# Scores of two prompt chunks from one stationary key tile per level, with the second chunk's keys and values in turned order

## What is computed

```python
def step(S, inp):
    qc, kc, vc, gc = inp
    b = jnp.cumsum(gc, axis=2)
    diff = b[:, :, :, None, :] - b[:, :, None, :, :]
    decay = jnp.exp(jnp.where(causal, diff, -jnp.inf))
    scores = jnp.einsum('bhtk,bhsk,bhtsk->bhts', qc, kc, decay)
    o = (jnp.einsum('bhts,bhsv->bhtv', scores, vc)
         + jnp.einsum('bhtk,bhkv->bhtv', qc * jnp.exp(b), S))
    b_last = b[:, :, -1:, :]
    S = (jnp.exp(b_last[:, :, 0, :])[..., None] * S
         + jnp.einsum('bhsk,bhsv->bhkv', kc * jnp.exp(b_last - b), vc))
    return S, o
```

## Time and profile before

| | us |
|---|---|
| median of 3 runs | 1489.78 (1488.51 to 1493.13) |
| the profiled execution, its own time | 1493.66 |
| span of that execution | 1491.4 |
| TensorE busy | 1460.7 |
| VectorE busy | 804.9 |
| ScalarE busy | 550.8 |
| GpSimd busy | 188.2 |

### The profile page before, as it was taken

How to read it: one execution, slowest core, us unless ns; L and a number is a source line. 1 busy time by engine, 2 the same in 40 slices (tenths; PEclk the granted TensorE clock), 3 DMA queues, 4 the chain that set the end, 5 groups by cost and what they waited for, 6 DMA issues and landing times.

```text
span 1491.4 us, 27027 instructions
## 1 busy us (share of the span) xinstructions
PE 1460.7 (98%) x9928; PEld 1440.6 (97%) x9928; DVE 804.9 (54%) x1200; ACT 550.8 (37%) x823; POOL 188.2 (13%) x202
## 2 busy tenths in 40 slices
PE   7999999999999999999999999999999999999996
PEld 5999999999999999999999999999999999999996
DVE  4657788787665554444444444444444444444443
ACT  6443433344443343333333333333333333333443
POOL 0244434333112210000000000000000000000131
PEclk9999999999999999999999999999999999999998
DMA  8445444434455555554565555565554556555453
GB/s 222 136 127 143 128 127 131 114 114 138 114 162 143 153 144 153 141 160 125 146 187 142 141 142 141 144 164 153 157 141 134 151 146 164 154 151 141 119 148 114
DMA packets 409519, 214.52 MB, mean 144 GB/s; under 512 B 4093, under 2 KB 407757, under 8 KB 409420
## 3 DMA queue, kind: packets, MB, share of 16 engines
q1 hardware_dynamic: 391207, 203.52, 49.8%
q10 hardware_dynamic: 18277, 10.52, 2.5%
HBM read 206.14 MB, written 7.89 MB: 144 GB/s over the span
## 4 chain that ended last, share of the span: by engine, by line
PE 85%; DVE 9%; issue 3%; ACT 2%; DMA 1%; DVEq 0%; ACTq 0%; SPq 0%
PE bank L366 27%; PE bank L367 27%; PE bank L368 27%; DVE qr L1190 2%; DVE w_lo L1013 2%; DVE t L1177 1%; ACT w_hi L682 1%; DVE sc L1205 1%; PE bank L507 1%; DMA xt<-in_x_sample 1%; DVE sn L1249 0%; PE bank L462 0%; PE bank L410 0%; PE bank L538 0%; PE bank L412 0%
## 5 line engine op out<-in xcount | busy, mean ns | idle before, releaser
L366 PE MATMUL bank<-a_hi,w_hi 128*128 128x320 f32 x2048 | 642.4, 314 | 0.0
L367 PE MATMUL bank<-a_lo,w_hi 128*128 128x320 f32 x2048 | 636.1, 311 | 0.0
L368 PE MATMUL bank<-a_hi,w_lo 128*128 128x320 f32 x2048 | 635.9, 311 | 0.0
L1013 DVE TENSOR_TENSOR w_lo<-w_raw,w_hi 128x1024 fp32r<-128x1024 f32 (+1 forms) x416 | 467.3, 1164 | 150.3 <-ACT w_hi L682 149.5
L682 ACT ACTIVATE w_hi<-w_raw 128x1024 fp32r<-128x1024 f32 (+1 forms) x416 | 387.3, 967 | 158.6 <-PE bank L368 148.5
L366 PEld LDWEIGHTS bank<-a_hi,w_hi 128*128 128x128 f32 x2048 | 387.6, 189 | 2.4
L367 PEld LDWEIGHTS bank<-a_lo,w_hi 128*128 128x128 f32 x2048 | 387.7, 189 | 0.8
L368 PEld LDWEIGHTS bank<-a_hi,w_lo 128*128 128x128 f32 x2048 | 387.3, 189 | 0.0
L366 PE MATMUL bank<-h_hi,w_hi 128*128 128x320 f32 x704 | 217.7, 309 | 0.0
L367 PE MATMUL bank<-h_lo,w_hi 128*128 128x320 f32 x704 | 216.6, 308 | 0.0
L368 PE MATMUL bank<-h_hi,w_lo 128*128 128x320 f32 x704 | 216.5, 308 | 0.0
(11 more groups left out here) (218 smaller groups left out, 1186.5 us busy)
## 6 DMA issues: line engine op xcount, KB each, us to landing
w_raw<-in_w_gate SPq DMA_DIRECT2D x44, 1024.0 KB, 5.6
w_raw<-in_w_up SPq DMA_DIRECT2D x44, 1024.0 KB, 5.6
w_raw<-in_w_down SPq DMA_DIRECT2D x64, 704.0 KB, 4.8
w_raw<-in_w_in SPq DMA_DIRECT2D x39, 1024.0 KB, 5.8
w_raw<-in_w_o SPq DMA_DIRECT2D x16, 1024.0 KB, 6.1
s<-in_state_hgrn ACTq DMA_DIRECT2D x8, 512.0 KB, 4.3
out<-sn ACTq DMA_DIRECT2D x8, 512.0 KB, 7.2
xt<-in_x_prompt SPq DMA_DIRECT2D x3, 512.0 KB, 9.4
```

The costliest lines, as they stand in the source:

```text
L366: pe.matmul(out, whi[:, par_, cols], r_hi, start=(k == 0), stop=False)
L367: pe.matmul(out, whi[:, par_, cols], r_lo, start=False, stop=False)
L368: last = pe.matmul(out, wlo[:, par_, cols], r_hi, start=False, stop=(k == last_k))
L1013: dve.tensor_tensor(wlo[:, par_, cols], raw[:, par_, cols], whi[:, par_, cols].bitcast(F32), SUB)\
```

## The change

The second chunk's keys and values are kept in turned (reversed) order, by GpSimd (`second_turned` in `keys`) and VectorE (`turned`, in place of one `scaled` into `vv`). In the turned chunk the first block of each pair comes second, so the 64 valid key columns of chunk 0 and the 64 of chunk 1 fill one tile of 128 columns without overlap. A new tile `km[l]` holds them. TensorE makes one product per level, `km[l]` stationary and 128 query columns moving, in place of two with 64. The mask table holds turned rows for chunk 1, and the put on the diagonal takes a turned identity from `cst`. GpSimd now keeps prompt keys in one tile `kp` that is multiplied in place, in the first blocks only (the second blocks' factor was 1), and the sample tokens' keys in `ks[l]`.

```diff
@@ rec_scores on TensorE
                 def level(bk, at, l):
-                    for c in range(NC):
-                        last = pe.matmul(bk[:, at + c * 64:at + c * 64 + 64].rearrange("p (m j) -> p m j", j=2 ** l),
-                                         kx[l][:, c * CH:(c + 1) * CH], right_half(qr[l][:, c * CH:(c + 1) * CH], l),
-                                         start=True, stop=True)
-                    return last
+                    return pe.matmul(bk[:, at:at + P].rearrange("p (m j) -> p m j", j=2 ** l),
+                                     km[l][:, :], right_half(qr[l][:, 0:TP], l), start=True, stop=True)
@@ the value projection on VectorE
+            def turned(n, par_):
+
+                done(n)
+                z = zb[par_]
+                dve.tensor_tensor(vv[:, 0:CH], z[:, 0:CH], rbc[:, 0:CH], MUL)
+                dve.tensor_tensor(second_turned(vv), z[:, CH:TP], rbc[:, CH:TP], MUL)
+                return dve.tensor_tensor(vv[:, TP:N], z[:, TP:N], rbc[:, TP:N], MUL)
...
-                    scaled(n + 2, par_, vv[:, :]).then_inc(unit_read, 1)
+                    turned(n + 2, par_).then_inc(unit_read, 1)
@@ keys on GpSimd
-                pool.tensor_tensor(kx[0][:, :].rearrange("p (m a) -> p m a", a=2),
-                                   ones[:, 0:1].unsqueeze(2).to_broadcast([P, N // 2, 2]), tl[0][:, :, 1:3], SUB)\
-                    .then_inc(kx_ready, 1)
+                spans = [(lambda ap: ap[:, 0:CH], 0, CH, 0), (second_turned, CH, CH, 1)]
+                for part, t0, n in [s[:3] for s in spans] + [(lambda ap: ap[:, TP:N], TP, NS)]:
+                    last = pool.tensor_tensor(part(kx0).rearrange("p (m a) -> p m a", a=2),
+                                              ones[:, 0:1].unsqueeze(2).to_broadcast([P, n // 2, 2]),
+                                              tl[0][:, t0 // 2:(t0 + n) // 2, 1:3], SUB)
+                last.then_inc(kx_ready, 1)
                 for l in range(LP):
-                    n = N if l < LS else TP
+                    src, m = (kp if l else kx0), CH // 2 ** (l + 1)
+                    one = ones[:, 0:1].unsqueeze(2).to_broadcast([P, m, 2 ** l])
                     pool.wait_ge(kx_ready, (LP + 1) * h + l + 1)
+                    for c in range(NC):
+                        last = pool.tensor_tensor(half_of(km[l][:, :], l, c), half_of(src[:, c * CH:(c + 1) * CH], l, c),
+                                                  one, MUL)
+                    last.then_inc(km_ready, 1)
                     if l:
                         pool.wait_ge(prod_ready, LP * h + l)
-                    pool.tensor_tensor(blocks_of(kx[l + 1], l, n), blocks_of(kx[l], l, n), times(l, n, 2), MUL)\
-                        .then_inc(kx_ready, 1)
+                        pool.wait_ge(km_ready, LP * h + l + 1)
+                    for part, t0, n, c in spans:
+                        if l:
+                            firsts = half_of(part(kp), l, 0)
+                            last = pool.tensor_tensor(firsts, firsts,
+                                                      tl[l][:, c * m:(c + 1) * m, 2:3].to_broadcast([P, m, 2 ** l]), MUL)
+                        else:
+                            last = pool.tensor_tensor(blocks_of(part(kp), 0, CH), blocks_of(part(kx0), 0, CH),
+                                                      times(0, CH, 2, t0), MUL)
+                    if l < LS:
+                        last = pool.tensor_tensor(blocks_of(ks[l + 1], l, NS), blocks_of(ks[l], l, NS),
+                                                  times(l, NS, 2, TP), MUL)
+                    last.then_inc(kx_ready, 1)
```

More of the change, by code:

```diff
@@ L54 @@
 C_ID = 0
-C_MP = C_ID + P
+C_AI = C_ID + P
+C_MP = C_AI + P
 C_MS = C_MP + LP * P
@@ L81, in constant_table @@
         for ch in range(NC):
-            c[:, C_MP + level * P + ch * 64:C_MP + level * P + ch * 64 + 64] = m
+            c[:, C_MP + level * P + ch * 64:C_MP + level * P + ch * 64 + 64] = m[::-1] if ch else m
         if level < LS:
@@ L162, in hybrid_kernel @@
         qr = region(early, [(f"qr{l}", [P, N if l <= LS else TP], F32) for l in range(LP + 1)])
-        kx = region(early, [(f"kx{l}", [P, N if l <= LS else TP], F32) for l in range(LP + 1)])
+        kx0, kp = region(early, [("kx0", [P, N], F32), ("kp", [P, TP], F32)])
+        km = region(early, [(f"km{l}", [P, CH], F32) for l in range(LP)])
+        ks = [kx0[:, TP:N]] + [t[:, :] for t in region(early, [(f"ks{l}", [P, NS], F32) for l in range(1, LS + 1)])]
         junk, = passing([("junk", [P, 1024], BF16)])
@@ L214, in hybrid_kernel @@
             sem(n) for n in ("pool_mm", "mp_hi_s", "mp_lo_s", "st_tr", "st_copied", "out_done"))
-        zf_sig, f_ready, prod_ready, zq_sig, q_ready, qr_ready, kx_ready = (
+        zf_sig, f_ready, prod_ready, zq_sig, q_ready, qr_ready, kx_ready, km_ready = (
             sem(n) for n in ("zf_sig", "f_ready", "prod_ready", "zq_sig", "q_ready",
-                             "qr_ready", "kx_ready"))
+                             "qr_ready", "kx_ready", "km_ready"))
         v_tr, k_tr, vt_ready, kt_ready, vm_ready, sc_mm, sc_put, put_go = (
@@ L259, in blocks_of, with times @@
             return ap[:, 0:n].rearrange("p (m a j) -> p m a j", a=2, j=2 ** level)
-        def times(level, n, lo):
-            m = n // 2 ** (level + 1)
-            return tl[level][:, 0:m, lo:lo + 2].unsqueeze(3).to_broadcast([P, m, 2, 2 ** level])
+        def times(level, n, lo, t0=0):
+            m, m0 = n // 2 ** (level + 1), t0 // 2 ** (level + 1)
+            return tl[level][:, m0:m0 + m, lo:lo + 2].unsqueeze(3).to_broadcast([P, m, 2, 2 ** level])
         def prod_in(level, which):
@@ L269, in prod_in, with second_turned, half_of @@
             return tl[level][:, 0:m, which:which + 1].rearrange("p (m a) q -> p m (a q)", a=2)
+        def second_turned(ap):
+            return ap[:, CH:TP][:, ::-1]
+        def half_of(ap, level, a):
+            return ap.rearrange("p (m a j) -> p m a j", a=2, j=2 ** level)[:, :, a, :]
         def right_half(ap, level):
@@ L513, in rec_scores @@
                 last.then_inc(sc_mm, 1)
[L514 to L517, removed]
+                for c, own in enumerate((kx0[:, 0:CH], kx0[:, CH:TP])):
+                    pe.matmul(SA[:, c * CH:(c + 1) * CH], own, qq[:, c * CH:(c + 1) * CH], start=True, stop=True)
+                last = pe.matmul(SA[0:NS, TP:N], ks[0], qq[:, TP:N], start=True, stop=True)
                 for l in range(LS):
                     last = pe.matmul(SA[0:NS, N + 32 * l:N + 32 * l + 32].rearrange("p (m j) -> p m j", j=2 ** l),
-                                     kx[l][:, TP:N], right_half(qr[l][:, TP:N], l), start=True, stop=True)
+                                     ks[l], right_half(qr[l][:, TP:N], l), start=True, stop=True)
                 last.then_inc(sc_mm, 1)
@@ L1320, in window @@
                     done(n + 2)
-                    out, src = thrice(v_rep, zb[par_])
-                    dve.tensor_tensor(out, src, thrice(v_rep, rbc)[1], MUL).then_inc(v_thrice, 1)
-                    scaled(n + 2, par_, vv[:, :]).then_inc(unit_read, 1)
+                    out, src = thrice(v_rep, zb[par_][:, TP:N])
+                    dve.tensor_tensor(out, src, thrice(v_rep, rbc[:, TP:N])[1], MUL).then_inc(v_thrice, 1)
+                    turned(n + 2, par_).then_inc(unit_read, 1)
                 else:
@@ L1508, in key_copies @@
                 after(pool, obc_mm, h)
-                out, src = thrice(k_rep, kx[LS])
+                out, src = thrice(k_rep, ks[LS])
                 one = ones[:, 0:2].unsqueeze(2).unsqueeze(3).to_broadcast([P, 2, 3, HS])
```

11 lines of the change are left out of this document (6 added, 5 removed).

## The result

The changed kernel takes 1505.05 us (median of 4 runs, 1503.06 to 1506.13) against 1491.45 (4 runs, 1488.51 to 1493.17): 1.0092 of the time before, with an interval of 1.0069 to 1.0114. It is slower by 0.9%, some 13.6 us, where 3.9% and 59 us were forecast (1549, with a range of 1508 to 1577). The measured time lies 3 us under the lower end of that range. The profiled execution of after has a span of 1502.1 us, 10.7 more than that of before.

What follows compares the result with a forecast made beforehand. VectorE and ScalarE in turns were taken to set the steady heads' period. Seven periods at 7.7 us gave 54, plus 6.7 for the first head, minus 1.3 on TensorE: +59 us on 1489.8, so 1549, range 1508 to 1577.

Steps and rivals of the forecast that it cites:

- The saving of 1.3 us a head on TensorE: TensorE's level products: 1.1 to 1.6 us saved a head, hidden in holes except in the last head, -1.3 us.
- the 0.15 us for `vv`: VectorE: one `vv` of 320 columns becomes three; two more instructions cost 0.15 us a head, on the path.
- the one from `kx0` to `q_ready` at 262.9: GpSimd's chain from keys to query tile: `q_ready` at 262.9, so VectorE starts `queries` 6.7 us later than at 256.18.
- The price of a short step: GpSimd's multiplies: 0.36 us on 64 columns, 0.16 us per own wait; levels 1 to 6 and `qq` 12.2 us.
- What stands in the way: VectorE's `t`, `w_lo` and norm steps hold up GpSimd from level 1 to `qq`, about 4 us.
- The start of level 1: GpSimd's `kx0` and level 0 fill 241.32 to 246.7; level 1 begins at 246.7, when `products` has its first result.
- relief for VectorE: VectorE's steps beside GpSimd's shorter ones: no gain was counted.
- sn in the queries: GpSimd's `k_rep` and `sn` both fall into VectorE's `queries`, 0.8 us a head more.
- the slow stretch: TensorE's lower clock behind its longer waits: 0 to 1 us a head, taken as 0, with 8 us kept for range.
- TensorE's waits: TensorE's holes grow to some 5 us ahead of the diagonal (L397) and 5 ahead of the level products.
- The milder rival: GpSimd's short steps cost 0.15 to 0.2 us, `q_ready` at 258 to 259, 1508 to 1520; chance 0.18.
- the hidden rival's condition: GpSimd's 26 added steps and 7 waits must cost under 2.5 us together; then 1479, chance 0.04.

Runs made afterwards that it cites:

- run 3: Changed kernel with GpSimd's query (`qq`) issued ahead of level 4 of keys, not behind level 6: 1467.02 us, ratio 0.9828.
- run 4: Changed kernel with copies into `km` on level 0 alone, TensorE using `km[0]` on every level (scores not the reference's): 1479.25 us, ratio 0.9913.
- run 5: Kernel before with GpSimd's eight key steps cut into 36 of 64 columns, nothing left out: 1515.03 us, ratio 1.0168.
- run 8: Changed kernel with query ahead of level 4 and each level's product cut back into two of 64 columns: 1484.2 us, ratio 0.9947.
- run 6: Kernel before with one added wait, so GpSimd's `sn` starts after VectorE's first put of that head: 1480.89 us, ratio 0.9925.
- run 7: Changed kernel with an added wait so `sn` starts after VectorE's first put, query left in place: 1491.1 us, ratio 0.999.
- run 1: Kernel before with one 128-column product per level, chunk 0's keys serving both chunks (scores not the reference's): 1486.93 us, ratio 0.9967.
- run 2: Changed kernel with each level's product cut back into two of 64 query columns on the same `km` tile: 1520.55 us, ratio 1.0194.
- run 10: Changed kernel with query ahead of level 4 and `sn` behind VectorE's first put: 1466.75 us, ratio 0.9825.

## Why the prediction was wrong, and where it was right

**Right: the direction and the mechanism.** `qq` became late, VectorE waited for it in every head, 2.6 us in the steady ones and 6.0 in the first, and short steps on GpSimd are the cause (runs 3, 4, 5). The saving of 1.3 us a head on TensorE was sized rightly (run 8), and so were the 0.15 us for `vv`.

**Wrong: the size.** The step that failed is the one from `kx0` to `q_ready` at 262.9. A head was to cost 7.7 us: 6.7 for `q_ready`, 0.8 for `sn` and `k_rep` in `queries`, 0.15 for `vv`. A steady head cost 1.4, and the mean of the seven was 1.1. Laid on the forecast's clock, `q_ready` came at 257.3 (16.0 us behind the start of `keys`, not 21.6). These 5.6 us are made up of three parts:
- *The price of a short step, 3.2 us.* 0.36 us for 64 columns was taken from a line through 192 and 320 columns. Measured: 0.28. The wait between own steps was taken at 0.16; it was 0.08 here. A level of four steps took 1.28 us and not 1.76. From level 1 to `qq` this is 9.0 us of work, and not 12.2.
- *What stands in the way, 1.7 us.* 4 us were forecast behind level 1 for VectorE's steps; it was 2.3 (2.7 in the head shown first). The two pieces of `w_lo` cost 1.8 to 1.9, near the forecast's 2.0, but the short norm steps next to nothing (0.16 us at 225.04, in the midst of GpSimd's steps) and `products` some tenths.
- *The start of level 1, 0.7 us.* Its first key step began 4.7 us behind the start of `keys` and not 5.4.

**A term at nothing: relief for VectorE.** Shorter instructions on one engine shorten the other's waits, since each waits for a whole instruction of the other. It was 1.1 to 1.3 us a head in `products` and 1.3 in the weight rests (mean 1276 ns, before 1498); run 5 shows both with the steps cut alone. The forecast kept VectorE's steps at their old length. But this did not make its sum wrong by some 2.5 us: 1.5 of them go into the wait for `qq`, 0.5 into the new wait for ScalarE's norm factors, and the rest into small steps. It is what made run 4 faster than the kernel before, and a part of what made run 3 so.

**Also too high: sn in the queries.** It was counted as a further 0.8 us. It was there before at 1.5 us a head (run 6), and `queries` grew by 0.1. Taking it out of the changed kernel is worth 14 us (run 7), which no term of the prediction looked at.

**TensorE: right for the kernel before, incomplete for the kernel after.** That the saving goes into holes holds before the change: in run 1 steady heads are as long as before. But the change itself made TensorE wait 2 to 3 us, its clock fell, and with 14 products its work in the slow stretch was on the chain; without the saving the changed kernel would be at 1520 (run 2). So the saving is worth 15.5 us there and not 1.3. The forecast priced the slow stretch at 0 with the saving in place, and that is nearly what was measured: steady heads took 35.2 us at a granted clock of 0.95 and 35.4 at 1.00, and one (the head shown first, where VectorE waited for TensorE) was 0.6 longer. This point therefore does not explain the miss. TensorE's waits were overrated like the rest: 5 us were forecast ahead of the level products and 2.2 to 3.4 measured in the steady heads, 5 ahead of the diagonal (L408) and 1.0 measured, in one head.

The milder rival had the wait for `qq` at the right end, with `q_ready` at 258 to 259 and a time of 1508 or more. It still lay above the measured one, and it got there in part by prices that were too low (0.15 to 0.2 us a step). A small slip: the change adds six waits on GpSimd, not the seven of the hidden rival's condition, which hardly moves it.

The gain of the change and the loss from order are of the same size, and the order decides: 1505 as it is, 1467 with one call moved.

## What to carry to other kernels

Where two engines exclude each other by whole instructions, cut steps cost the one their fixed part and give the other its time back: count both sides, ask whether the time given back is waited away again, and look at which step stands beside the long chain of the other. When a producer is cut into more steps, look first at what is queued behind it in its engine's order and who waits for that; moving one call may be worth more than the change. A saving on an engine with holes is not nothing if the holes lower its clock: ask what it does just behind them.

## What the runs showed of the hardware

- GpSimd's multiply on 64 columns took 0.28 us in a row of two, on 128 columns 0.40 to 0.47, on 320 columns 0.72 to 0.88. By the shortest and the longest, some 0.17 us of it do not depend on the columns, an estimate.
- Where both engines wanted the tiles they went in turns, as the prediction had assumed. Beside two pieces of `w_lo` directly behind each other, each of two key steps waited for one piece (1.15 and 1.27 us, where 0.28 is the undisturbed step), so that a pair with 0.56 us of work took 2.39. The other way round the pieces took 1.34 and 1.31 us beside short steps, where they took 1.22 alone, and 1.91 beside a 128x320 step (243.20, before).
- With waits of 2 to 3 us ahead of the scores TensorE's granted clock over a head was 0.84 to 0.94, and 1.00 in another head with nearly the same wait. Behind the same wait of 3.97 us it was back at 1.00 by 136 us with seven products of 128 columns, and still at 0.50 with fourteen of 64 (run 2). The heads of run 3 have no wait and stood at 1.00 throughout, though 2.19 us of waiting (L507) lie just ahead of the first; with 2.21 us there run 10 showed 0.95 in its first head, and with 2.45 run 8 showed 0.87. Run 8 showed 0.95 in two further heads with no wait listed.
